# Weaving the q and k blocks of two attention layers between the attention steps

## The chip, the cores and the metric

The kernel runs on one core of one Trainium2 chip. The metric is device microseconds from the start to the end of one launch, and lower is better. TensorE (PE) multiplies matrices, VectorE (DVE) and ScalarE (ACT) work elementwise, GpSimd (POOL) issues the transfers of the small and streamed tables, and SyncE (SP) issues the transfers of the large weights. All data are float32.

## The reference

A transformer of two layers over 256 tokens of width 1024 is followed by a second network that the change does not touch. Each layer conditions its input, mixes tokens and runs a mixture of 32 experts:

```
mod = silu(c) @ ada_w[i] + ada_b[i]            # six rows of 1024: shift, scale, gate, twice
h   = rms_norm(x) * (1 + scale1) + shift1
q, k, v = split(h @ w_in, 3)                    # w_in is 1024 x 3072
y   = attention(q, k, v) @ w_out
x   = x + gate1 * y
h   = rms_norm(x) * (1 + scale2) + shift2
x   = x + gate2 * moe(h)                        # top 2 of 32 experts
```

Layer 0 uses differential attention: 8 heads, two softmax maps for each head, a chunk-causal mask, and 16 (head, query tile) pairs. Layer 1 uses stick-breaking attention with 16 heads: sigmoids and a reversed running sum of logarithms in place of a softmax.

## The kernel before

**Storage.** `ring` has six slots of 2 MB, and SP fills them in a written order; a slot is filled again when PE has counted its last use (`free(n)`). The eight 512-column slices of a layer's `w_in` and `w_out` are ring items 0 to 7 of the layer, behind them come the gate, up and down weights of the experts. `ada_in` holds three buffers of 1 MB for the rows of `ada_w` and `w_mod_2`. POOL loads them (`ada_load`, L1484), and they are called ada items here: items 0 to 31 belong to layer 0, items 32 to 63 to layer 1, eight items to a group. Item i can be loaded when the buffer of item i - 3 has been used.

**Groups of items.** In groups 1, 2, 5 and 6 (`SUMMED`) DVE multiplies each item by its column of `cond` and adds it to a running sum (`ada_sum`, L1851), and PE adds up the partitions once, at the group's last item. In the other groups PE multiplies each item itself (`ada_item`, L2181). When a group is through, `ada_take` adds the bias and POOL stores the row.

**Head (0 to 40 us).** SP loads the first 2048 columns of `ada_w` as eight pieces of 1 MB, with the constants and x behind the third, and then the weights. PE multiplies all eight pieces, turns `h`, and after `first_line` turns the row of shift and scale into columns (`first_norm`, L1864). ACT then writes `hT` (`take_hT`, L1659).

**q, k, v (`qkv`, L2215).** Twelve blocks of 16 matmuls: four of q, four of k, four of v. A block of q or k has two half blocks of 128 columns. ACT copies each block out of one of four banks (`take_qkv`, L1677). In the meantime DVE runs both sums of the layer. Only then do the attention steps begin.

**Attention steps.** `diff_attention` (L2275) runs 20 steps. Step k computes scores k, turns the probabilities of k - 3 and multiplies k - 4 by v, and twelve of the steps carry an ada item. `stick_attention` (L2317) runs 18 steps: scores k, running sums k - 1, product k - 2, with an item in 14 of them. Scores, exponentials and the division pass from PE to DVE (`diff_scores`, `diff_combine`, L1912) and ACT and back.

**Behind them.** `projection` (L2251) multiplies by `w_out` in four blocks of eight products; three items in layer 0 and two in layer 1 follow it, then come the turned x, the router (item 31 in layer 0) and the experts. SP holds back the experts' weights of layer 0 until 24 items are used, and the early down weights until 32 (layer 1: 64) are used. In layer 1 the context row of the second network is loaded by POOL when x is complete, and ACT squares it before the exponentials of the router.

## Time and profile before

| what | us |
|---|---|
| median of three runs (lowest, highest) | 1855.09 (1849.57, 1863.38) |
| the profiled execution, its span | 1853.06, 1851.3 |
| head, until the first block of q | 0 to 39.85 |
| q, k, v and both sums, layer 0 | 39.85 to 127.15 |
| attention steps, layer 0 | 127.15 to 185.04 |
| projection, layer 0 | 185.04 to 213.3 |
| its items, turned x, router | 213.3 to 243.12 |
| experts, layer 0 | 243.12 to about 727 |
| q, k, v, layer 1 | 733.81 to 827.67 |
| attention steps, layer 1 | 827.67 to 893.52 |
| projection, layer 1 | 893.52 to 921.78 |
| its items, turned x, router | 921.78 to 953.36 |
| experts of layer 1 with the second network, rest | 953.36 to 1851.3 |

The borders are starts of PE instructions in the trace. A row of the timeline gives the start, the time, the engine, the line of the kernel, the output and inputs, the number of instructions, and in brackets the idle time ahead of it with what ended it. L2179 is the helper that issues every matmul, so its rows are told apart by shape: 128x256 for half blocks, 128x512 with `ring` for v and the projection, `small` or `cst` with 128*1 or 128*2 for an ada item.

### The profile page before, as it was taken

The numbers are of one execution on the slowest core, as the hardware profiler recorded it, in microseconds if no ns is written. First come the engines' busy times: TensorE is split into PE (matmuls) and PEld (weight loads), VectorE is DVE, ScalarE is ACT, GpSimd is POOL, SyncE is SP. The second block draws the span as 40 slices with busy tenths as digits, with TensorE's granted clock in tenths as the row PEclk, the third lists the DMA queues.
The fourth block names the chain that finished last, engine by engine and source line by source line (L and its number), as shares of the span: only waits on it lengthen the run. The fifth ranks groups of instructions, "written<-read, shape, count | busy, mean of one in ns | idle before, by whom it ended". The sixth has DMA issues, their size and how long they took to land.

```text
span 1851.3 us, 18408 instructions
## 1 busy us (share of the span) xinstructions
PE 1687.5 (91%) x7485; PEld 858.7 (46%) x7485; DVE 489.6 (26%) x931; ACT 444.1 (24%) x939; POOL 158.1 (9%) x235
## 2 busy tenths in 40 slices
PE   5997999889888878989999999999998899989988
PEld 2843543333333334835464444444443356565564
DVE  1357220000000103244241002221120123553362
ACT  2015221111111102015231112334331034343351
POOL 2012010000000010113000010000000000100000
PEclk9998999999989999999989999999998999999999
DMA  9999779999999999987369989999999962413310
GB/s 348 360 350 401 277 278 419 421 421 420 421 421 419 420 413 397 338 349 239 109 259 389 369 298 404 393 414 420 420 420 409 377 230 100 148 53 117 137 46 24
DMA packets 119488, 585.12 MB, mean 316 GB/s; under 512 B 11744, under 2 KB 16680, under 8 KB 94720
## 3 DMA queue, kind: packets, MB, share of 16 engines
q1 hardware_dynamic: 97776, 489.59, 66.0%
q0 software_dynamic: 21504, 88.72, 13.1%
q10 hardware_dynamic: 112, 5.51, 0.8%
q8 instruction: 63, 1.03, 0.2%
q14 instruction: 33, 0.27, 0.0%
HBM read 578.87 MB, written 21.32 MB: 324 GB/s over the span
## 4 chain that ended last, share of the span: by engine, by line
PE 58%; DMA 29%; DVE 6%; ACT 3%; issue 3%; SPq 1%; ACTq 0%; DVEq 0%
PE psum L2179 55%; DMA ring<-in_expert_w_up 20%; DMA work<-in_ada_w 4%; DMA ring<-in_diff_w_in 2%; DVE work L1859 1%; PE psum L697 1%; DMA ring<-in_expert_w_gate 1%; DMA work<-in_ctx 1%; DMA work<-in_w_mod 1%; DVE small L1055 1%; PE psum L2418 1%; PE psum L1196 1%; DMA ring<-in_w_out 0%; DVE work L2147 0%; DVE work L2074 0%
## 5 line engine op out<-in xcount | busy, mean ns | idle before, releaser
L2179 PE MATMUL psum<-ring,work 128*64 128x512 f32 (+5 forms) x4272 | 1092.6, 574 | 69.6 <-DMA ring<-in_expert_w_up 56.3
L2179 PEld LDWEIGHTS psum<-ring,work 128*64 128x64 f32 (+2 forms) x4272 | 422.7, 152 | 666.1 <-issue 638.0
L2179 PE MATMUL psum<-work 128*128 128x192 f32 (+9 forms) x1048 | 220.4, 375 | 8.5 <-DVE work L2007 3.0
L2179 PEld LDWEIGHTS psum<-work 128*128 128x128 f32 (+3 forms) x1048 | 146.5, 191 | 108.0 <-issue 86.9
L2074 DVE TENSOR_TENSOR work<-work,psum 128x256 f32<-128x256 f32 x64 | 26.9, 421 | 593.2 <-ACT work L1779 593.2
L1779 ACT ACTIVATE work<-psum 128x256 f32<-128x256 f32 x64 | 24.5, 383 | 607.4 <-PE psum L2179 607.4
L2179 PE MATMUL psum<-work,ring 128*128 128x256 f32 x704 | 156.1, 381 | 3.5 <-DMA ring<-in_diff_w_in 2.0
L2179 PEld LDWEIGHTS psum<-work,ring 128*128 128x128 f32 x704 | 132.0, 190 | 27.8 <-issue 7.0
L1646 ACT ACTIVATE work<-psum 128x256 f32<-128x256 f32 (+5 forms) x184 | 79.7, 443 | 225.0 <-PE psum L2418 76.0
L1545 POOL DMA_INDIRECT expert_rows<-work,targets x56 | 55.1, 984 | 807.1 <-DVE work L2100 807.1
L2100 DVE TENSOR_TENSOR work<-psum,rows 128x512 f32<-128x512 f32 x64 | 44.3, 692 | 255.8 <-PE psum L2179 255.7
L1859 DVE SCALAR_TENSOR_TENSOR work<-work,small 128x2048 f32<-128x2048 f32 x28 | 65.8, 2352 | 80.2 <-DMA work<-in_ada_w 79.7
L1730 ACT ACTIVATE work<-psum,small 128x192 f32<-128x192 f32 x128 | 58.4, 506 | 25.5 <-PE psum L2179 25.5
L1646 ACT ACTIVATE ring<-psum 128x512 f32<-128x512 f32 (+2 forms) x54 | 34.5, 640 | 54.0 <-PE psum L2179 41.0
L2179 PE MATMUL psum<-work,cst 128*128 128x128 f32 (+4 forms) x176 | 30.2, 384 | 13.4 <-DVE work L2149 6.2
L697 PE MATMUL psum<-cst 128*128 128x256 f32 x166 | 42.2, 407 | 0.0
L1491 POOL DMA_DIRECT2D work<-in_ada_w x40 | 22.8, 574 | 215.5 <-DVE work L1859 162.1
L2179 PE MATMUL psum<-work,small 128*2 128x512 f32 (+1 forms) x256 | 38.2, 682 | 2.1 <-DMA work<-in_ada_w 1.2
L2418 PE MATMUL psum<-cst,work 128*128 128x128 f32 x128 | 27.3, 295 | 13.0 <-DVE work L2074 12.9
L697 PEld LDWEIGHTS psum<-cst 128*128 128x128 f32 x166 | 32.8, 205 | 12.0 <-issue 7.5
L1684 ACT ACTIVATE work<-psum 128x512 f32<-128x512 f32 x16 | 9.6, 597 | 104.9 <-PEq L2235 53.5
L1055 DVE TENSOR_REDUCE small<-psum 128x1 f32<-128x512 f32 (+1 forms) x48 | 28.7, 599 | 21.2 <-PE psum L2179 20.4
(293 smaller groups left out, 956.3 us busy)
## 6 DMA issues: line engine op xcount, KB each, us to landing
ring<-in_expert_w_gate SPq DMA_DIRECT2D x60, 2048.0 KB, 16.5
ring<-in_expert_w_up SPq DMA_DIRECT2D x60, 2048.0 KB, 17.2
ring<-in_expert_w_down SPq DMA_DIRECT2D x57, 2048.0 KB, 13.5
work<-in_ada_w POOLq DMA_DIRECT2D x40, 1024.0 KB, 8.0
ring<-in_w_in SPq DMA_DIRECT2D x12, 2048.0 KB, 8.8
work<-in_w_mod POOLq DMA_DIRECT2D x16, 1024.0 KB, 7.9
ring<-in_diff_w_in SPq DMA_DIRECT2D x6, 2048.0 KB, 38.2
ring<-in_sb_w_in SPq DMA_DIRECT2D x6, 2048.0 KB, 22.8
```

Of the source, the lines that this page charges most:

```text
L697: nc.tensor.matmul(bank[b][:, 0:S], ident, cst[:, 5 * P:7 * P], start=True, stop=True, skip_group_check=True)
L1055: V.tensor_reduce(nm2[:, k % 3:k % 3 + 1], score_bank(p, k)[:, 0:n * P], AX.X, ALU.max, negate=True).then_inc(sem("a_max"), 1)
L1491: pool.dma_start(ada_in[:, i % 3, 512 * k:512 * (k + n)], src[:, c * 512:(c + n) * 512].rearrange("(p t) n -> p t n", t=KT)[:, t, :]).then ...
L1545: pool.indirect_dma_start(expert_rows.rearrange("r (k n) -> (r k) n", k=2), bass.IndirectOffsetOnAxis(ap=targets[:, e:e + 1], axis=0), out ...
L1646: copy = lambda o_, i_: nc.scalar.activation(o_, i_, ACT.Copy)
L1730: ins = nc.scalar.activation(hS[:, c // QUAD % 2, t, 0:QUAD * LIST], bank[b][:, k * S:k * S + QUAD * LIST], ACT.Identity, scale=gain[:, t: ...
L1779: nc.scalar.activation(s_act, gu_bank(l, e)[:, 0:S], ACT.Silu).then_inc(sem("silu"), 1)
L1859: ins = V.scalar_tensor_tensor(now, now, cond[:, 0, t:t + 1], before, ALU.mult, ALU.add)
L2074: V.tensor_tensor(hid, s_act, gu_bank(l, e)[:, S:2 * S], ALU.mult).then_inc(sem("hid"), 1)
L2100: V.tensor_tensor(outb[:, e % 2, :], bank[down_bank(l, e)], gate2, ALU.mult).then_inc(sem("out_ev"), 1)
L2179: return T.matmul(out_, lhsT, rhs, start=start, stop=stop, skip_group_check=True)
L2418: ins = T.transpose(bank[2][:, j * P:(j + 1) * P], src[:, j * P:(j + 1) * P], ident)
```

## The change

- **Head.** x comes first. The first columns of `ada_w` come in two halves of their width, each in four pieces of two transfers (2 KB runs in place of 8 KB); between the halves SP loads the first four of eight row groups of the first two slices of v. PE makes the columns of half the row, starts all four v blocks with the first four products, and ends them with the second half of the row and of the weights.
- **Order.** The slices are loaded in the order v, v, q, k, q, k. Both layers compute v first, then the first pair of q and k blocks; the other 12 half blocks stand one at a time ahead of steps 0 to 11 of the attention. A step's scores wait for the pair that it needs.
- **Steps.** In layer 0 the steps 0 to 11 use one pair of score banks, turn probabilities 2 steps and multiply 3 steps after the scores; from step 12 it is two pairs, 3 and 4 steps as before. DVE combines k - 1 ahead of scores k up to step 12.
- **Items.** The first group of a layer (1, 5) is summed before the steps and used at step 0; the second (2, 6) is summed one item at a time in steps 1, 2, 4, 5, 7, 8, 10, 11 and used at step 12. Later items: 16 to 19 in steps 13 to 19, 20 and 21 behind them, 22 to 27 behind the first three projection blocks, 28 to 30 as before. Layer 1: 48 to 52 in steps 13 to 17, 53 behind them, 54 to 59 behind three projection blocks, 60 behind the fourth, then 61, 62, 63.
- **Waits.** The second pair of q and k slices waits until six items are used. POOL's first three item loads wait for the last piece of the head's row instead of for the first turned columns; in exchange the loads of lambda and of the router come later.
- **Places.** The turned result of layer 1 goes in the place of `h`, which keeps `hT` readable during the steps; layer 0's squares go back to their bank.

```diff
-    oT = hT
+    oT = hT, h.rearrange("p t d -> p (t d)").rearrange("p (k s) -> p k s", k=KT)
+    SLICES = (4, 5, 0, 2, 1, 3)
+    V_BLOCKS = (0, 2, 1, 3)
+    WOVEN = 12
+    WEAVE_BANK = (2, 5)
+    SUM_AT = (1, 2, 4, 5, 7, 8, 10, 11)
+    def diff_bank(u):
+        return 2 * (u % 2) if u >= WOVEN else 0
...
+            if l == 0 and n == 4:
+                sp.wait_ge(sem("ada_used"), 6)
...
+        sp.dma_start(x[:], a["x"][0].rearrange("(t p) d -> p t d", p=P)).then_inc(sem("x_in"), 16)
+        for a_ in range(2):
+            for q in range(4):
+                for t in range(2):
+                    sp.dma_start(first_in(a_, q)[:, t * 1024:(t + 1) * 1024].rearrange("p (s n) -> p s n", s=2),
+                                 first[:, 2 * q + t, :, a_, :]).then_inc(sem(f"first_in{4 * a_ + q}"), 16)
+                if a_ == 0 and q == 1:
+                    sp.dma_start(cst[:], a["consts"]).then_inc(sem("consts"), 16)
+            if a_ == 0:
+                for n in range(2):
+                    w = a["diff_w_in"][0][:, SLICES[n] * 512:(SLICES[n] + 1) * 512].rearrange("(t p) n -> p t n", t=KT)
+                    sp.dma_start(wslot(L_BASE[0] + n, KT, 512)[:, 0:4, :], w[:, 0:4, :]).then_inc(sem("w_first"), 16)
...
+        pool.wait_ge(sem("first_in7"), 32)
+        for i in range(3):
+            ada_load(i)
+        pool.wait_ge(sem("first_mm"), 2)
...
-            for g in SUMMED[2 * l:2 * l + 2]:
-                ada_sum(g)
-                ada_take(g)
+            ada_sum(SUMMED[2 * l])
...
                 for k in range(16 + 2):
-                    if k == 11:
-                        ada_take(3)
+                    if 1 <= k <= WOVEN:
+                        diff_combine(k - 1)
                     if k < 16:
                         diff_scores(k)
-                    if k >= 2:
+                    if k >= WOVEN + 2:
                         diff_combine(k - 2)
+                    if k == 1:
+                        ada_take(1)
+                    if k in SUM_AT:
+                        ada_sum(2, [SUM_AT.index(k)])
+                    if k == WOVEN:
+                        ada_take(2)
...
             router_prep(l)
+            ada_take((3, 7)[l])
             update_x(2 * l, "proj_mm", v)
...
+        def woven_half(l, p, c):
+            j = (p - 4) // 2
+            out_ = bank[WEAVE_BANK[l] + p % 2][:, c * S:(c + 1) * S]
+            n = L_BASE[l] + 2 + p % 2 + 2 * (j // 2)
+            if c == 0:
+                loaded(pe, n)
+                pe.wait_ge(sem("qkv"), EACH["qkv"] * l + ((2, 4)[p % 2] if p < 6 else p - 1))
+            w = wslot(n, KT, 512)
+            col = j % 2 * 256 + c * P
+            for t in range(KT):
+                ins = mm(out_, w[:, t, col:col + P], hT[:, t, :], t == 0, t == KT - 1)
+            if c:
+                if j % 2:
+                    taken(ins, n)
+                else:
+                    ins.then_inc(sem("qkv_mm"), 1)
...
+        def head():
+            first_product(0, range(0, 4))
+            first_turn(range(0, 6))
+            first_product(0, range(4, 6))
+            keep_warm(0, 2)
+            first_product(0, range(6, KT))
+            first_cols(0)
+            keep_warm(0, 5)
+            for i, b in enumerate(V_BLOCKS):
+                v_part(0, b, range(0, 4))
+                if i == 0:
+                    first_turn(range(6, KT))
+                elif i == 1:
+                    first_product(1, range(0, KT))
+                elif i == 2:
+                    first_cols(1)
+        def front(l, ts):
+            for i, b in enumerate(V_BLOCKS):
...
+            for p in (4, 5):
+                for c in range(2):
+                    woven_half(l, p, c)
...
-        DIFF_ITEMS = share_out(16, [0, 0] + 8 * [1] + [0, 0] + 4 * [1, 0])
+        DIFF_ITEMS = [[KT - 1] if k == 0 else [2 * KT - 1] if k == WOVEN else [(k + 19) // 2] if k in (13, 15, 17, 19) else []
+                      for k in range(16 + 4)]
+        STICK_ITEMS = [[5 * KT - 1] if k == 0 else [6 * KT - 1] if k == WOVEN else [35 + k] if k > WOVEN else []
+                       for k in range(HEADS_S + 2)]
+        PROJ_ITEMS = [[22, 23], [24, 25], [26, 27], []], [[54, 55], [56, 57], [58, 59], [60]]
...
             for k in range(16 + 4):
+                if k < WOVEN:
+                    woven_half(0, 6 + k // 2, k % 2)
...
-            for i in (28, 29, 30) if l == 0 else (62, 63):
+            for i in (28, 29, 30) if l == 0 else (61, 62, 63):
                 ada_item(i)
```

## Rows read from the trace of the kernel before

**Rows 1.** The page, part 4: shares of the chain that ended last, by engine.

```profile
PE 58%; DMA 29%; DVE 6%; ACT 3%; issue 3%; SPq 1%; ACTq 0%; DVEq 0%
```

**Rows 2.** Stretches: us, busy (count) of PE, PEld, DVE, ACT, POOL; PEclk, DMA, GB/s.

```profile
0.00:39.85 39.85, 19.17 (x111) 7.94 (x111) 4.13 (x12) 8.53 (x16) 7.53 (x17) 1.00 0.94 338
...
39.85:80.00 40.15, 39.28 (x180) 33.98 (x181) 15.40 (x7) 3.77 (x7) 4.91 (x9) 1.00 1.04 392
...
127.15:160.20 33.05, 24.75 (x161) 10.46 (x161) 26.71 (x71) 18.52 (x83) 9.81 (x18) 0.85 0.98 378
...
185.04:213.30 28.26, 27.96 (x67) 12.33 (x68) 3.95 (x7) 2.73 (x4) 0.00 (x0) 1.00 0.70 261
...
280.00:699.00 419.00, 362.21 (x1590) 142.54 (x1586) 36.58 (x69) 44.69 (x106) 30.80 (x33) 0.96 1.01 419
...
893.52:921.78 28.26, 27.96 (x66) 12.33 (x67) 3.68 (x6) 2.73 (x4) 0.00 (x0) 1.00 0.00 1
```

**Rows 3.** Timelines of PE and POOL: start, us, engine, line, operation [idle before].

```profile
33.72 1.04 PE L2179 MATMUL psum<-ring,small 128*1 128x512 f32 x8
...
37.10 1.61 POOL L1491 DMA_DIRECT2D work<-in_ada_w  x3
```

**Rows 4.** Timeline of DVE, first layer: sums of one group, scores two steps apart.

```profile
44.97 1.29 DVE L1861 TENSOR_SCALAR work<-work,small 128x2048 f32<-128x2048 f32 x1 [8.12 <-DMA work<-in_ada_w]
...
81.42 2.35 DVE L1859 SCALAR_TENSOR_TENSOR work<-work,small 128x2048 f32<-128x2048 f32 x1 [4.82 <-DMA work<-in_ada_w]
...
132.66 0.42 DVE L1918 SCALAR_TENSOR_TENSOR work<-cst,psum 128x256 f32<-128x256 f32 x1
...
160.22 0.42 DVE L1918 SCALAR_TENSOR_TENSOR work<-cst,psum 128x256 f32<-128x256 f32 x1
```

**Rows 5.** Timeline of PE inside the steps of the first attention.

```profile
144.04 0.42 PE L2294 MATMUL psum<-cst,work 128*128 128x128 f32 x2 [0.86 <-DVE work L1934]
...
144.61 1.04 PE L2179 MATMUL psum<-work,small 128*1 128x512 f32 x8
...
145.58 0.70 PE L2179 MATMUL psum<-work 64*128 64x256 f32 x4
...
146.38 0.62 PE L2179 MATMUL psum<-work 128*128 128x128 f32 x4
...
148.64 0.49 PE L2179 MATMUL psum<-work 64*128 64x128 f32 x4
```

**Rows 6.** The chain of waits: start, us, what.

```profile
91.68 5.02 DMA work<-in_ada_w
...
214.66 12.35 DMA work<-in_w_mod
...
923.84 14.94 DMA work<-in_ctx
```

**Rows 7.** DMA issues of 140 to 190 us: count, KB, median us to landing.

```profile
work<-in_w_mod POOLq DMA_DIRECT2D x7, 1024.0 KB, 13.6
```

**Rows 8.** Timeline of SP's DMA issues.

```profile
153.75 0.34 SPq L1442 DMA_DIRECT2D ring<-in_expert_w_gate  x1
```

**Rows 9.** Timeline of PE, second layer: first block, then inside the steps.

```profile
733.81 14.15 PE L2179 MATMUL psum<-work,ring 128*128 128x256 f32 x64
...
846.95 0.92 PE L2179 MATMUL psum<-work 64*128 64x256 f32 x4
...
847.80 1.14 PE L2179 MATMUL psum<-work,cst 128*128 128x256 f32 x6
...
848.87 0.86 PE L2179 MATMUL psum<-work 128*64 128x256 f32 x4
...
866.36 1.14 PE L2179 MATMUL psum<-work,cst 128*128 128x256 f32 x6 [0.91 <-DVE work L2149]
...
870.32 1.14 PE L2179 MATMUL psum<-work,cst 128*128 128x256 f32 x6 [1.18 <-DVE work L2149]
...
873.16 0.92 PE L2179 MATMUL psum<-work 64*128 64x256 f32 x4
```

More of the change, by code:

```diff
@@ L1619, in _, with stick_act @@
         pool_second(pool)
-    def stick_act(act, link, copy):
+    def stick_act(act, link, copy, take_woven):
         act.preload_act_table_set("natural_log_exp_and_others")
+        for p in range(6):
+            take_woven(1, p)
         for k in range(HEADS_S + 2):
+            if k < WOVEN and k % 2:
+                take_woven(1, 6 + k // 2)
             if k < HEADS_S:
@@ L1795, in _ @@
             take_hT(2 * l)
-            take_qkv(l)
             if l == 0:
                 act.preload_act_table_set("natural_log_exp_and_others")
+                for p in range(6):
+                    take_woven(0, p)
                 act.wait_ge(sem("lam_dot"), 1)
@@ L1812, in _ @@
             else:
-                stick_act(act, link, copy)
+                stick_act(act, link, copy, take_woven)
             square_norm(2 * l + 1)
@@ L1849, in gain_cols, with ada_sum @@
             link(V.scalar_tensor_tensor(gain, gain, 1.0, g_, ALU.add, ALU.mult))
-        def ada_sum(g):
-            for t in range(KT):
+        def ada_sum(g, ts=range(KT)):
+            for t in ts:
                 i = KT * (g - 1) + t
@@ new lines, in first_product @@
+        def first_product(a_, ts):
+            for t in ts:
+                if t % 2 == 0:
+                    pe.wait_ge(sem(f"first_in{4 * a_ + t // 2}"), 32)
+                for k in range(4):
+                    ins = mm(bank[7][32 * k:32 * k + 1, a_ * S:(a_ + 1) * S], cond[:, 0, t:t + 1],
+                             first_in(a_, t // 2)[:, t % 2 * 1024 + k * S:t % 2 * 1024 + (k + 1) * S], t == 0, t == KT - 1)
+                if t % 4 == 3:
+                    ins.then_inc(free(2 * a_ + t // 4), 1)
@@ new lines, in first_turn, with first_cols @@
+        def first_turn(ts):
+            for t in ts:
+                for tile in range(TT):
+                    ins = T.transpose(bank[FIRST_TURN[t // 2]][:, (t % 2 * TT + tile) * P:(t % 2 * TT + tile + 1) * P],
+                                      h[:, tile, t * P:(t + 1) * P], ident)
+                if t % 2:
+                    ins.then_inc(sem("hT_mm"), 1)
+        def first_cols(a_):
+            pe.wait_ge(sem("first_line"), 2 * a_ + 1)
+            for i in range(2):
+                ins = T.transpose(bank[(3, 5)[a_]][:, i * P:(i + 1) * P], line[:, a_ * S + i * P:a_ * S + (i + 1) * P], ident)
+            ins.then_inc(sem("first_mm"), 1)
@@ new lines, in v_part, with taken @@
+        def v_part(l, b, ts):
+            w = wslot(L_BASE[l] + b % 2, KT, 512)
+            for t in ts:
+                if b == 0:
+                    pe.wait_ge(sem("hT_done"), HT_AT[2 * l] + t + 1)
+                ins = mm(bank[b][:], hT[:, t, b // 2 * P:(b // 2 + 1) * P], w[:, t, :], t == 0, t == KT - 1)
+            return ins
+        def taken(ins, n):
+            ins.then_inc(free(n), 1)
+            pe.wait_ge(free(n), turn_of(n) + 1)
+            pe.sem_inc(sem("qkv_mm"), 1)
+        def woven_half(l, p, c):
+            j = (p - 4) // 2
+            out_ = bank[WEAVE_BANK[l] + p % 2][:, c * S:(c + 1) * S]
[10 more added lines that the diff above has]
+                    taken(ins, n)
+                else:
+                    ins.then_inc(sem("qkv_mm"), 1)
@@ L2263, in projection @@
                     mm(bank[5][:, 0:NG + NX], C["ones"], kT[:, 2, 0:NG + NX], True, True).then_inc(sem("r_bias"), 1)
+                for n in PROJ_ITEMS[l][i]:
+                    ada_item(n)
             for hf in range(2):
@@ L2308, in diff_attention @@
                     ada_item(i)
+            for i in (20, 21):
+                ada_item(i)
             for j in range(4):
@@ L2562, in _ @@
                 transpose_h(2)
-            qkv(l)
+            front(l, range(0 if l else 4, KT))
             (diff_attention, stick_attention)[l]()
             projection(l)
-            for i in (28, 29, 30) if l == 0 else (62, 63):
+            for i in (28, 29, 30) if l == 0 else (61, 62, 63):
                 ada_item(i)
```

262 lines of the change are left out of this document (123 added, 139 removed).

## The prediction, made before the change was run

> **What bounds the kernel now.** I read the page's chain first: PE is 58% of what ended last and transfers 29% [rows 1]. So the same microsecond can belong to either, and it has to be asked stage by stage. The windows [rows 2] give the stages. The experts of layer 0 run at DMA share 1.01 and 419 GB/s while PE has 57 us idle in 419: that stage is paced by transfers, but its stream is tied to slots that PE frees, so it moves with the moment at which the experts begin. Ahead of it the stretch from 39.85 to 80 is full on both sides (PE 39.28 of 40.15 busy, DMA 1.04). The attention steps of layer 0 are full on neither: in 127.15 to 160.20 PE is busy 24.75 of 33.05 us with a mean clock of 0.85, so stretches of it run at the lower of the two levels, 1.2 GHz, behind idle time. That is the room the change aims at. The projection is PE alone: 27.96 of 28.26 us in both layers, with DMA 0.70 in the first and 0.00 in the second.
>
> **Units.** A block of q or k: 64 matmul records of four half blocks take 14.15 us, with the gap to the next some 14.2, so a half block is 3.55 us [rows 9]. One ada item holds PE for 0.97 us (144.61 to 145.58) [rows 5]. Two steps of the first attention hold PE, without the item, for 0.57 + 0.80 + 0.62 + 0.49 = 2.5 us, 1.24 a step [rows 5], while before they came 2.76 us apart (132.66 to 160.22 is ten steps) [rows 4]. In layer 1 a step holds PE for 0.85 + 1.07 + 0.79 = 2.71 us without its item, and two steps without an item came 3.96 apart (866.36 to 870.32), PE waiting 1.18 for DVE [rows 9].
>
> **Head, layer 0.** The first v products can start about ten us earlier, since half of the 4+4 MB of `ada_w` now suffices. That isn't what counts: the steps can't begin before group 1 is summed. POOL issued its first three loads at 37.10, 3.4 us behind PE's last head product [rows 3]. Now they wait for the last piece itself, which has 2.1 MB of v ahead of it: at 392 GB/s 5.4 us later, about 39.1. So the sums start 2 us later than at 44.97; they ended at 81.42 + 2.35 = 83.8 [rows 4]. Against this, SP has only 6.3 MB queued beside them, since the second pair of slices waits for six items. All that must have landed is some 27 MB (x 1.0, constants 0.9, the row 8.4, v 4.2, first q and k 4.2, eight items 8.4), and the old kernel had moved 13.5 + 15.7 = 29.2 MB by 80 us [rows 2], 27 by 75. The end of the sums thus lies between 77 and 86; I take 80, and 81.3 with item 7. PE has finished v, the first q and k blocks and one half block by then (28.4 + 14.2 + 3.55 from about 29, held up by weights), and idles in front of item 7. This idle time and the smaller transfers are not free: 1.5 us for the clock is set down below, between 0 and 4.
>
> **Woven steps, layer 0.** Step 1 starts at 81.3. Eleven steps hold PE for 3.55 + 1.24 = 4.8 us each. DVE needs about 2.4 us for scores and combination, 2.76 by the old pace as a bound, and 2.35 for a sum in eight of twelve steps: 5.1 in such a step, 4.3 in the mean, below PE's 4.8. I take PE's: 52.8, plus the 1.5. Step 12 starts at 135.6. From the scores of u = 12, at 160.2 before, to the projection at 185.04 it was 24.8, with 0.5 for PE's part 25.3. The end of the attention is then 160.9, **24 us earlier**.
>
> **What goes the other way.** Six of the items that stood in steps, 22 to 27, now stand in the projection: 5.8 us. This leaves 18.3. These items also wait for transfers. An item's load can't be issued before the third last is used, and what it takes depends on company: 5.02 us alone at 91.68, 12.35 beside the two expert loads behind the projection [rows 6], a median of 13.6 beside four expert loads and the 5.4 MB of expert rows [rows 7]. Those four loads went out at 153.75, 31 us ahead of the projection [rows 8], because 24 items were used; now item 23 is behind the first projection block, so they start in it, together with the expert rows and eight items: 5.4 + 8.4 + 7.3 MB, then 4.2 + 4.2 more, 29.5 MB or 70 us at 419 GB/s from 161 on. Followed block by block with 8 to 15 us for a load, PE waits 1 us at item 25, 5 at 27, 4 at 30, less for shorter loads: 3 to 11 us, I take 8. The experts' weights are in by 231 to 235, just when they are wanted. **Layer 0: 24 - 6 - 8 = 10 us.**
>
> **Layer 1.** v takes 28.4 and the first pair 14.2 from 733.81: 776.4. Item 39 is ready by then: DVE begins its group when the last rows of layer 0 are added, before 734, and eight sums took 38.8 us in layer 0. Step 0 is 3.55 + 0.85 + 0.97, step 1 is 3.55 + 0.85 + 1.07, ten steps of 6.26: 850. There ACT's and DVE's chain of 3.96 fits under 6.26, and even with a sum in DVE's queue. From step 12 to the projection it was 873.16 to 893.52, 20.4 us; with two more items and the wait for the last sum 23.5. The projection starts at 873.5, **20 us earlier**. Six items in it cost 6: its end comes 14 us earlier. Here DMA is idle, so their loads come in time at 5 us.
>
> The exception is the last. Item 60 now stands behind the fourth block, and the load of item 63 waits for it. It goes out about 1.6 us after the projection's end, beside the two expert loads that this end releases. That is the very company of the load that took 12.35. So PE is held until 14 us behind the projection, done at 14.9; before, its two items were done after 2.1. The turned x and the router stand behind. Of these 12.8 us some 1.7 are free, since the router's end was waiting for the context row (923.84, 14.94 us [rows 6]) and ACT's work on it (from the projection to the first expert layer 1 took 31.6 us, layer 0 with two more items 29.8). The cost is 11 (between 4 with a load of 5.02 and 14 with one of 14.94, that of the context row). **Layer 1: 14 - 11 = 3 us.**
>
> **Other edits,** each at nothing. Turning layer 1's results into h's place: the same ACT copy. Squares in PSUM: same count. The loads of lambda, router and norm rows come later but are wanted at 80 and 160; if norm rows came behind 168 the projection's bias product would wait. SP's twelve extra issues lie ahead of transfers that are queued anyway. 2 KB runs: up to 1 us in the head.
>
> **Sum.** 10 + 3 = 13 us off the profiled execution's 1853.06 gives 1840; this lies 2 us under the median of the runs, so I say **1842**. Under 1%, 18.5 us, a measurement of this kernel can't well tell from no change.
>
> **Rivals.**
> - **The items' loads don't hold PE.** If they land in about 5 us even in company, layer 0 keeps 18.3 - 3 = 15 and layer 1 14 - 4 = 10: 25 us, 1830. For it speaks the 5.02 us of a load without company [rows 6] and that three loads can be under way; against it the 12.35 and the median of 13.6 [rows 6, 7].
>  The Trainium skill ("DMA: Bandwidth & Descriptors", section "Queues, rings and completion order") says that each DMA engine takes turns between the queues that have work, a packet at a time; by that, 1 MB on POOL's queue beside SP's would be in after about 2 MB, near 5 us. The 12.35 us of the trace [rows 6] do not agree.
> - **The half blocks lengthen the steps (slower).** PE's queue is in order, and so is DVE's: a late half block holds the next scores, a late sum the next combination. If nothing overlaps, a step lasts 3.55 + 2.76 = 6.3 in layer 0 and 3.55 + 3.96 = 7.5 in layer 1: 11 x 1.5 + 10 x 1.25 = 29 us; with half of the 16 sums of 2.35 in series 19 more: 1890. It makes the kernel slower by over 1% once a step grows by more than (13 + 18.5) / 21 = 1.5 us. Against it: scores k + 1 need only DVE's scores k, a half block earlier.
> - **Transfers set the end.** If the experts' stream, and not PE, decides when layer 0 goes on, its later start (behind item 23) gives all 10 us back, and late loads the other 3: 1855. Against it: the old stream was idle for 0.30 of the projection [rows 2], which the new order fills.
>
> **Chances.** Forecast 0.56, short loads 0.23, longer steps 0.09, transfers 0.12. The range 1825 to 1859 takes in the third rival, most of the first, and the bounds of head (-3 to +6) and stalls (-12 to +6); outside lie the slow rival and the lower end of the first. Faster by over 1%: 0.21 of the first rival and 0.06 of the forecast's low end, 0.27. Slower: 0.07 of the slow rival. Within: 0.66.
>
> **What would show it.** DVE's last sum of group 1 at 78 to 83; half blocks 4.8 us apart in layer 0 and 6.3 in layer 1, PE at 1.00 there; the first projection at 161; items 25, 27 and 30 each behind a DMA wait, and one wait of over 10 us for `w_mod` behind the second projection. It would be wrong if the sums end after 86, if step distances exceed 5.5 and 7, or if item 63 waits under 5 us.

## The result: slower by 0.8%, and the profile after

| | us |
|---|---|
| kernel before, median of 7 runs (lowest, highest) | 1855.09 (1849.57, 1863.38) |
| changed kernel, median of 7 runs | 1868.04 (1866.37, 1873.02) |
| ratio, 95% interval | 1.0078 (1.0062 to 1.0093) |
| profiled execution of the changed kernel, its span | 1866.77, 1865.0 |

The forecast was 1842 us, with a range of 1825 to 1859. The span grew by 13.7 us instead of shrinking by 13. Against the table of before, from the trace of after:

| stage | start before | start after | forecast |
|---|---|---|---|
| projection, layer 0 | 185.04 | 169.45 | 160.9 |
| first expert, layer 0 | 243.12 | 253.69 | 233 |
| v, layer 1 | 733.81 | 743.71 | |
| projection, layer 1 (from v) | 893.52 (159.7) | 889.08 (145.4) | (139.7) |
| first expert, layer 1 | 953.36 | 966.42 | |

So layer 0 was 15.6 us ahead at its projection and 10.6 behind at its experts: 26 us went between the two, a stretch that took 58.1 us before and takes 84.2 now. From v to the first expert layer 1 took 222.7 us, before 219.6: another 3. Behind that nothing changed (898.6 us to the end, before 897.9). These are two single executions. Two kernels below differ from the changed one in layer 1 alone, and their traces have the projection of layer 0 at 173.64 and 171.81 and the first expert at 258.92 and 257.50, so a start in layer 0 is only good to some 5 us; the stretch from projection to first expert is steadier (84.2, 85.3 and 85.7).

The page's chain, shares by engine; it answers to [rows 1] and hardly tells the two kernels apart:

```profile
PE 62%; DMA 28%; DVE 4%; SPq 2%; issue 2%; ACT 2%; POOL 0%; ACTq 0%; DVEq 0%
```

The windows of the changed kernel (columns as in [rows 2]): the head's second part, two slices of it, woven steps, projection with its items in layer 0, PE's longest hole in it, the experts, projection with its items in layer 1.

```profile
39.85:80.00 40.15, 30.26 (x88) 16.83 (x87) 13.95 (x10) 6.20 (x10) 8.78 (x15) 0.89 0.94 311
...
60.00:70.00 10.00, 7.40 (x33) 6.00 (x32) 2.10 (x1) 1.20 (x2) 0.53 (x1) 1.00 0.94 234
70.00:80.00 10.00, 2.87 (x7) 2.31 (x8) 5.12 (x3) 0.00 (x0) 1.06 (x2) 0.57 0.67 217
...
91.30:127.00 35.70, 35.09 (x182) 28.09 (x179) 26.53 (x49) 13.78 (x57) 4.25 (x7) 1.00 0.59 215
...
169.45:226.70 57.25, 41.23 (x139) 14.58 (x139) 6.01 (x8) 3.68 (x5) 5.49 (x10) 0.85 0.98 382
...
186.60:197.68 11.08, 0.00 (x1) 0.00 (x2) 1.08 (x1) 2.73 (x4) 0.55 (x1) 0.70 0.97 367
...
280.00:699.00 419.00, 367.62 (x1622) 145.61 (x1618) 37.04 (x71) 46.44 (x110) 31.81 (x34) 0.96 1.01 417
...
889.08:936.60 47.52, 39.30 (x151) 14.22 (x147) 6.00 (x8) 4.17 (x7) 9.93 (x18) 0.93 0.71 274
```

Three things stand here. The stretch to 80 us was full on both sides before (39.28 of 40.15, 392 GB/s [rows 2]) and now has 30.26 and 311. The woven steps are what the change was meant to give: PE 35.09 of 35.70 at clock 1.00, with DMA only 0.59 busy, so bandwidth is left over there. And the projection of layer 0 is the reverse: PE 41.23 of 57.25 at 0.85 with DMA 0.98. The work that transfers do was not spread with the work that PE does.

PE's timeline, layer 0: the k block (48 products in one row), half blocks in steps, then the projection with the waits at its items 25 and 27.

```profile
77.13 12.87 PE L2241 MATMUL psum<-work,ring 128*128 128x256 f32 x48 [9.43 <-DMA ring<-in_diff_w_in]
...
109.85 3.62 PE L2241 MATMUL psum<-work,ring 128*128 128x256 f32 x16
...
114.53 3.62 PE L2241 MATMUL psum<-work,ring 128*128 128x256 f32 x16
...
169.45 7.13 PE L2241 MATMUL psum<-ring,work 128*128 128x512 f32 x16 [1.21 <-ACT work L1763]
...
197.68 1.89 PE L2241 MATMUL psum<-work,small 128*2 128x512 f32 x8 [11.08 <-DMA work<-in_w_mod]
199.50 7.95 PE L2241 MATMUL psum<-ring,work 128*128 128x512 f32 x16
...
213.05 1.89 PE L2241 MATMUL psum<-work,small 128*2 128x512 f32 x8 [4.63 <-DMA work<-in_w_mod]
214.86 8.79 PE L2241 MATMUL psum<-ring,work 128*128 128x512 f32 x16
```

Behind each wait PE runs "cold", at the lower of its two clock levels for a while: the granted clock is 0.50 in the item right behind each wait (197.68 to 199.50 and 213.05 to 214.86), which takes 1.8 us for 1.0, and 0.89 and 0.81 over the blocks that follow, which take 7.95 and 8.79 us for 7.13. Item 30 (in the row 223.96) has no wait. DVE's timeline, the fifth and the last of the eight sums of group 1, which answer to the 81.42 of [rows 4]; the chain of waits in both projections, which answers to [rows 6]; and the DMA issues of 170 to 200 us (columns as in [rows 7]):

```profile
70.35 2.35 DVE L1909 SCALAR_TENSOR_TENSOR work<-work,small 128x2048 f32<-128x2048 f32 x1 [8.25 <-DMA work<-in_ada_w]
...
86.86 2.35 DVE L1909 SCALAR_TENSOR_TENSOR work<-work,small 128x2048 f32<-128x2048 f32 x1 [4.92 <-DMA work<-in_ada_w]
```

```profile
186.93 26.08 DMA work<-in_w_mod
...
225.32 12.72 DMA work<-in_w_mod
...
882.30 4.92 DMA work<-in_w_mod
...
925.11 9.57 DMA work<-in_w_mod
```

```profile
work<-in_w_mod POOLq DMA_DIRECT2D x4, 1024.0 KB, 23.1
ring<-in_expert_w_gate SPq DMA_DIRECT2D x2, 2048.0 KB, 25.9
ring<-in_expert_w_up SPq DMA_DIRECT2D x2, 2048.0 KB, 33.0
```

A load of 1 MB took 5.02 us alone and 13.6 in the old crowd [rows 6, 7]; in the new one the median of four is 23.1. That of item 25, issued at 178.03, was in when PE went on at 197.68, after 19.65 us; that of item 27, issued at 186.93, was in 26.08 us later, but it had item 26's ahead of it on POOL's own queue. Who had the DMA engines meanwhile stands in the queues of 178 to 198 us (packets, MB, share): ACT's with the expert rows, SP's, and POOL's with the items.

```profile
q10 hardware_dynamic: 67, 2.92, 40.3%
q1 hardware_dynamic: 175, 2.61, 34.6%
q0 software_dynamic: 179, 1.33, 18.3%
```

POOL's queue has as many packets through as SP's (179 and 175), but 7.4 KB in each against 15, and 44 for ACT's. So it moves 1.33 MB of 6.86, 67 GB/s. ACT's count is lower because its copy runs out in this window. While all three had work, in 183 to 188 us, the three counts are near equal:

```profile
q10 hardware_dynamic: 21, 1.20, 65.5%
q1 hardware_dynamic: 25, 0.41, 27.0%
q0 software_dynamic: 22, 0.18, 11.7%
```

POOL has 36 GB/s there. With ACT's copy out of the way, in 193 to 203 us, it is 193 packets of SP's and 188 of POOL's, and POOL has 138 GB/s, or 7.6 us for an item. PE takes two items per block there, one in 4.5 us. Last, PE in layer 1: the wait at item 53, the projection, and item 63.

```profile
887.26 1.89 PE L2241 MATMUL psum<-work,small 128*2 128x512 f32 x8 [3.88 <-DMA work<-in_w_mod]
889.08 7.90 PE L2241 MATMUL psum<-ring,work 128*128 128x512 f32 x16
...
934.72 1.89 PE L2241 MATMUL psum<-work,small 128*2 128x512 f32 x8 [8.22 <-DMA work<-in_w_mod]
```

### The profile page after: what moved, and what is told of

Same layout as the page of the kernel before. It is cut to its first block, busy times and chain, and to the rows that moved or that the text cites. A ratio compares the mean times of both kernels' runs of the same rounds, so it can differ in the third digit from the quotient of the medians.

```text
span 1865.0 us, 18564 instructions
## 1 busy us (share of the span) xinstructions
PE 1684.4 (90%) x7537; PEld 858.5 (46%) x7537; DVE 488.6 (26%) x935; ACT 446.2 (24%) x939; POOL 158.1 (8%) x236
## 3 DMA queue, kind: packets, MB, share of 16 engines
q0 software_dynamic: 21536, 88.72, 12.9%
q8 instruction: 64, 1.05, 0.2%
## 4 chain that ended last, share of the span: by engine, by line
PE 62%; DMA 28%; DVE 4%; SPq 2%; issue 2%; ACT 2%; POOL 0%; ACTq 0%; DVEq 0%
PE psum L2241 58%; DMA ring<-in_expert_w_up 20%; DMA work<-in_w_mod 3%; DMA ring<-in_diff_w_in 2%; PE psum L713 1%; SPq L1416 1%; DMA ring<-in_expert_w_gate 1%; DMA ring<-in_expert_w_down 1%; DVE small L1071 1%; PE psum L2555 1%; PE psum L1212 1%; DMA mod_scratch<-rows 0%; SPq L1406 0%; DMA ring<-in_w_out 0%; SPq L1447 0%
## 5 line engine op out<-in xcount | busy, mean ns | idle before, releaser
L2241 PE MATMUL psum<-work,ring 128*128 128x256 f32 x704 | 161.4, 385 | 10.0 <-DMA ring<-in_diff_w_in 9.4
L2555 PE MATMUL psum<-cst,work 128*128 128x128 f32 x128 | 27.3, 295 | 13.0 <-DVE work L2127 12.9
L713 PE MATMUL psum<-cst 128*128 128x256 f32 x154 | 38.1, 402 | 0.0
L1696 ACT ACTIVATE work<-x 128x1024 f32<-128x1024 f32 x10 | 10.5, 1055 | 109.5 <-DVE x L1954 93.9
```

The source lines that it names most:

```text
L713: nc.tensor.matmul(bank[b][:, 0:S], ident, cst[:, 5 * P:7 * P], start=True, stop=True, skip_group_check=True)
L2241: return T.matmul(out_, lhsT, rhs, start=start, stop=stop, skip_group_check=True)
L2555: ins = T.transpose(bank[2][:, j * P:(j + 1) * P], src[:, j * P:(j + 1) * P], ident)
```

## The experiments

The kernel before was timed anew beside each group of kernels: 1854.79, 1855.07, 1853.84 and 1856.14 us. The ratios below, with their 95% intervals, are to those, and 1.0078 (1.0062 to 1.0093) is the changed kernel's.

**1. Only the six items moved, in the kernel before.** Items 22 to 27 leave the steps and stand behind the first three projection blocks of layer 0; nothing is woven.

```diff
-        DIFF_ITEMS = share_out(16, [0, 0] + 8 * [1] + [0, 0] + 4 * [1, 0])
+        DIFF_ITEMS = share_out(16, [0, 0] + 6 * [1] + 12 * [0])
+        PROJ_ITEMS = [[22, 23], [24, 25], [26, 27], []], [[], [], [], []]
```

> The kernel before the change with one part of it: items 22 to 27 of layer 0 stand behind the first three projection blocks in place of in the attention steps, and group 3 is taken behind the steps; so SP's wait for 24 items ends in the projection too. Theory (moving these items costs more than it gives, because their loads meet the experts' weights and rows): six items of 1 us and waits of 12 to 20 us in the projection, against some 5 us less in the steps: 10 to 20 us slower than before, 1865 to 1875. Rival (the cost comes only from attention ending earlier while the transfers are not further on): under 6 us, 1855 to 1861.

Measured: 1874.18, 1.0103 (1.0085 to 1.0121). PE's timeline in the projection:

```profile
207.51 1.89 PE L2179 MATMUL psum<-work,small 128*2 128x512 f32 x8 [9.32 <-DMA work<-in_w_mod]
...
222.91 1.89 PE L2179 MATMUL psum<-work,small 128*2 128x512 f32 x8 [4.31 <-DMA work<-in_w_mod]
```

The waits of the changed kernel are there without any weaving. The move alone costs 19 us, as expected: from the projection to the first expert it is 82.8 us for 58.1, and the steps that it empties give back only 4 (projection at 181.04 for 185.04). In the changed kernel the woven half blocks earn part of it back.

**2. The same products, hardly any bytes.** In the changed kernel the loads of items 22 to 30 carry 64 columns of each piece of up to 2048; the rest of these rows is left out.

```diff
+                wide = 64 if 22 <= i <= 30 else n * 512
-                pool.dma_start(ada_in[:, i % 3, 512 * k:512 * (k + n)],
+                pool.dma_start(ada_in[:, i % 3, 512 * k:512 * k + wide],
```

> The changed kernel, with the loads of items 22 to 30 cut to 64 of 512 columns in each section, one eighth of their bytes; it leaves out most of those rows of w_mod, while the products, waits and signals stay as they are. It separates the price of the transfers from that of the items' products on PE. Theory (PE waits 11.08 and 4.63 us at items 25 and 27 for bytes, and its blocks behind them run cold for another 2 to 3 us): both waits fall under 2 us and the time is 1848 to 1855 us. Rival (what holds PE is that only three buffers stand between an item and its load, so latency and POOL's turn decide, not bytes): the wait at item 25 stays above 6 us and the time at 1862 to 1868.

Measured: 1849.73, 0.9975 (0.9959 to 0.999), 18 us under the changed kernel. One number in the expectation is off: the trace shows that 32 KB were left of 1024, not one eighth.

```profile
work<-in_w_mod POOLq DMA_DIRECT2D x6, 32.0 KB, 6.4
```

PE's wait at item 25 fell from 11.08 to 1.76 us and the one at 27 vanished. The first expert starts at 237.15, 16.5 us earlier than in the changed kernel and 6 before the old one. From the projection to the first expert it is 58.1 us in the kernel before, 84.2 in the changed one and 66.9 here. So 17.3 of the 26.2 us lost were paid for bytes, with products, buffers and POOL's order all in place; 5.8 are the six items' products, and 3 are left, about what PE waits at items 25 and 31 (1.76 and 1.68). Small loads are not free in this crowd either: those of 32 KB took 6.4 us. This kernel also changes the size of POOL's packets and leaves their number, and the counts stay equal beside SP's queue (186 to 190 us):

```profile
q1 hardware_dynamic: 51, 0.84, 56.7%
q0 software_dynamic: 52, 0.03, 2.7%
```

**3. The crowd thinned from either end.** SP's wait for 24 items ahead of the experts' weights is taken out (first kernel); or the 5.4 MB of expert rows go out at step 2 of the attention instead of ahead of the projection (second); or the first, and `w_out` waits for 8 items instead of 13 (third).

```diff
-            if l == 0:
-                sp.wait_ge(sem("ada_used"), KT * 3)
...
+                    if k == 2:
+                        act.dma_start(expert_rows, finite).then_inc(sem("rows_set"), 16)
...
-                sp.wait_ge(sem("ada_used"), KT * 2 - 3)
+                sp.wait_ge(sem("ada_used"), KT)
```

> The changed kernel without SP's wait for 24 used items ahead of the experts' weights of layer 0. Theory (the loads of the moved items hold PE in the first projection, because four expert loads and the expert rows start in it; item 25 waited 11.1 us and item 27 4.6 us): the four expert loads go out from about 127 us on, into the stretch where DMA was only 0.59 busy, the two waits shrink to under 8 us in sum and the kernel gets 6 to 12 us faster than the changed one (1868): 1856 to 1862. Rival (the three item buffers alone set the pace of the items, whatever else is queued): the waits stay over 12 us and the time stays at 1866 to 1870.

> The changed kernel with ACT's copy of 5.4 MB into expert_rows issued at step 2 of the first attention (about 97 us) in place of right before the first projection. Theory: it leaves the crowded stretch, 13 us of DMA time less there; the waits at items 25 and 27 fall by 5 to 12 us: 1856 to 1863. Rival (SP's four expert loads alone are enough to fill the stretch, and the copy only takes what is left over): under 3 us, 1865 to 1870. If the sums of group 2 wait for transfers because of it, the woven steps grow beyond 4.7 us.

> The changed kernel without the wait for 24 items ahead of the experts' weights, and with w_out already behind 8 used items instead of 13. The first of these alone moved the crowd to steps 12 to 19 (waits of 1.5 to 3.5 us at six items, projection 18.5 us later) and won nothing. Theory (layer 0 ends where the transfers end: 20 MB must pass between 127 us and the experts, while DMA is only 0.59 busy from 91 to 127): w_out and the first two expert loads now pass in that gap, 8.4 MB or 20 us of transfers leave the crowd, and the experts start 8 to 18 us earlier: 1850 to 1860. Rival (the waits of the items come from three buffers and not from company): no gain, 1866 to 1872.

Measured: 1871.54 (1.0097, 1.0077 to 1.0116), 1868.17 (1.0081, 1.006 to 1.0101) and 1861.63 (1.0041, 1.0026 to 1.0057). The first two gained nothing against the changed kernel, and the third gained 6.4 us, less than the 8 to 18 expected. In the first, the four loads went out at 126 to 140 and met items 16 to 21 instead; two of PE's six waits in and behind the steps, and the one left in the projection:

```profile
160.15 1.89 PE L2239 MATMUL psum<-work,small 128*1 128x512 f32 x8 [3.55 <-DMA work<-in_ada_w]
...
167.52 1.89 PE L2239 MATMUL psum<-work,small 128*1 128x512 f32 x8 [3.49 <-DMA work<-in_ada_w]
...
210.51 1.89 PE L2239 MATMUL psum<-work,small 128*2 128x512 f32 x8 [5.39 <-DMA work<-in_w_mod]
```

Its projection starts at 187.98, 18.5 us later than in the changed kernel. In the second the wait at item 25 is gone, but in the steps from 110 to 127 PE is busy for only 13.40 of 17 us (17.00 in the changed kernel), and 4.27 us at item 27 stay. Its projection starts 4.75 later than the changed kernel's, which is no more than single executions differ by. In the third the loads go out from 91 us on, into the woven steps, where the changed kernel had DMA at 0.59. There PE reads nothing from POOL's queue except sums for DVE, which have slack.

**4. Two places outside the projection.** POOL issues the router's loads at item 9 instead of item 4 (first); item 60 stands behind the third block of layer 1's projection, so that item 63's load goes out a block earlier (second); and both (third).

```diff
-                if i == 4:
+                if i == 9:
                     router_load(0)
...
-        PROJ_ITEMS = ..., [[54, 55], [56, 57], [58, 59], [60]]
+        PROJ_ITEMS = ..., [[54, 55], [56, 57], [58, 59, 60], []]
```

> The changed kernel with the loads of the first router (runs of 16 to 128 bytes) behind item 9 in place of item 4. Theory (these short runs hold the DMA engines between 60 and 70 us, where DMA moves 234 GB/s at share 0.94, so that item 4's load takes 15 us and k's first slice lands only at 77.1): the sums of group 1 end at 80 to 85 in place of 89.2, the woven steps start 4 to 9 us earlier, the kernel is 2 to 8 us faster: 1860 to 1866. Rival (the total of bytes and three buffers set the end of the sums): they end at 88 to 90, no difference.

> The changed kernel with item 60 behind the third projection block of layer 1 in place of behind the fourth, so that the load of item 63 can start 7 us earlier, before the two expert loads. Theory: the wait of 8.2 us at item 63 goes, and with it the cold clock behind it: 7 to 11 us faster, 1857 to 1861. Rival (the router then waits for the context row and ACT as before the change): 3 us or less, 1865 to 1868.

> The changed kernel with only the two repairs that won alone: item 60 behind the third block (9.8 us) and the router's loads behind item 9 (7.4 us). They sit in different layers; the sum is expected: 1848 to 1854, equal to before or a little faster. If layer 0's gain were only a shift that the transfers take back, 1856 to 1860.

Measured: 1860.67 (1.0031, 1.0016 to 1.0046), 1858.26 (1.0021, 1.0008 to 1.0034), 1854.51 (0.9996, 0.9982 to 1.001). Windows of the first, for the two slices shown above of after, and PE behind layer 1's projection in the second:

```profile
60.00:70.00 10.00, 7.51 (x33) 6.01 (x32) 2.47 (x2) 1.19 (x2) 0.53 (x1) 1.00 0.89 289
70.00:80.00 10.00, 6.70 (x22) 5.60 (x23) 6.73 (x3) 0.00 (x0) 1.05 (x2) 0.66 0.72 246
```

```profile
929.87 2.76 PE L2241 MATMUL psum<-work,small 128*2 128x512 f32 x24 [0.30 <-PE psum L2241]
```

The router's four loads of 2 to 128 KB stood on POOL's queue right behind item 4's. Later, the same ten microseconds move 289 GB/s for 234, k's slice is in at 73.30 for 77.13, and the last sum ends at 86.4 for 89.2, not at 80 to 85 as expected. The rate is no accident of one trace: all seven traces of kernels with these loads at item 4 have 230 to 259 GB/s in 60 to 70 us, and all nine with them at item 9 have 289 to 309. How 2.8 us at the sums become 7 in the end was not followed. With item 60 earlier the 8.22 us wait is gone, and from the projection of layer 1 to its first expert it is 66.6 us for 77.3. The two gains (7 and 10 us) add up to 13.5, not 17.

**5. All of these together** (`w_out` and the experts' weights early, router late, item 60 earlier), and then variants of it. In the second kernel the expert rows go out on ACT's queue behind the first norm. In the third POOL also issues the loads of items 21 and 53 ahead of its wait for the scratch rows; in the fourth, items 22, 23 | 24 | 25, 26, 27 stand behind the projection blocks.

```diff
+                if n == 1 and t == 0:
+                    act.dma_start(expert_rows, finite).then_inc(sem("rows_set"), 16)
...
-                if g > LAST0 * l and i % 8 == 4:
+                if g > LAST0 * l and i % 8 == (5 if g in (2, 6) else 4):
                     stored(g)
...
-        PROJ_ITEMS = [[22, 23], [24, 25], [26, 27], []], ...
+        PROJ_ITEMS = [[22, 23], [24], [25, 26, 27], []], ...
```

> g_wout together with item 60 behind the third block (alone 9.8 us) and the router's loads behind item 9 (alone 7.4 us). Theory: the three repairs sit in different stretches (layer 1's projection, group 1's sums, the crowd of layer 0) and add up: 1832 to 1843, faster than before. Rival (layer 0 ends where its transfers end, so two repairs of layer 0 overlap): router and w_out together give no more than the larger: 1840 to 1850.

> The kernel of the last combination (router loads late, w_out and the experts' weights early, item 60 earlier) gave 1850.6 us and still waits 5.09 us for the load of item 25 in the first projection, with a cold block behind it. The 5.4 MB of expert rows go out just ahead of that projection. Here they go out on ACT's queue about 12 us later, behind the first norm, where that kernel's DMA was about half busy. Theory (company on the queues sets how long a w_mod load takes): the wait at item 25 falls to under 1 us, its block runs warm, 1843 to 1848 us. Rival (the crowd just moves, as it did when the experts' weights went early): a wait of 3 us or more appears at items 27 to 31 or at the router instead, 1849 to 1853.

> As the kernel with late expert rows, and POOL issues the store and the bias and norm loads of groups 2 and 6 one item later, so that the loads of items 21 and 53 go out first (before, POOL waits 8.66 us for the scratch rows ahead of item 53's load, and PE waits 4.38 at item 21 and 4.04 at item 53). Theory: POOL's order of issue is what delays them; both waits fall under 1 us and the time goes 4 to 8 us below that kernel: 1837 to 1843. Rival (item 21's load is late because of company alone, and behind item 53 something else is late by as much): 0 to 3 us less.

> As the kernel before it in this call, with items 22, 23 | 24 | 25, 26, 27 behind the first three projection blocks of layer 0 instead of 22, 23 | 24, 25 | 26, 27: item 25 has one block (7 us) longer for its load. Theory: what is left of the wait at item 25 goes and nothing comes at 27, since the loads ahead of it are issued when items 22 to 24 are done: 0 to 5 us less than that kernel. Rival: the wait only moves to item 26 or 27, because loads 26 and 27 are issued when 23 and 24 are used and 24 is no earlier: no difference within 0.1%.

Measured: 1850.59 (0.9977, 0.9967 to 0.9986), 1865.46 (1.0051, 1.0033 to 1.0069), 1860.87 (1.0028, 1.0013 to 1.0044) and 1860.4 (1.0034, 1.0021 to 1.0047). The first missed its 1832 to 1843: its repairs meet each other in the steps from 127 to 140, where PE is busy for 8.24 of 13 us at 402 GB/s (11.73 with only the weights early). Late rows were wrong: the wait at item 25 went and this came, at items 28, 29 and 31 of the second kernel:

```profile
209.55 1.04 PE L2240 MATMUL psum<-work,small 128*2 128x512 f32 x8 [1.45 <-DMA work<-in_w_mod]
...
224.78 1.89 PE L2240 MATMUL psum<-work,small 128*2 128x512 f32 x8 [14.20 <-DMA work<-in_w_mod]
...
232.12 1.89 PE L2240 MATMUL psum<-work,small 128*2 128x512 f32 x8 [5.46 <-DMA work<-in_w_mod]
```

Items 28 to 30 are the last before the router, and have no block between them to hide a load; item 29's load, issued at 200.50, had the expert rows beside it and then two expert loads of 2 MB (208.22). The queues of 194 to 214 us:

```profile
q10 hardware_dynamic: 96, 5.51, 77.0%
q0 software_dynamic: 283, 1.86, 23.2%
```

POOL's order in the third takes 4.6 us off the second, near what was expected of it, though its total was missed with the base: from v to layer 1's projection it is 141.8 us for 145.8. The places of the items in the fourth change nothing while that hole stands.

**6. POOL's order and item 25, each alone.** The move of item 53's load in the changed kernel (first) and in the combination (second); item 21's as well (third); the second with the items in the places 22, 23 | 24 | 25, 26, 27 (fourth). The edits are those above, with `g == 6` in place of `g in (2, 6)` where it is item 53 alone.

> The changed kernel, with one edit in layer 1: POOL issues the load of item 53 ahead of its wait for the scratch rows of group 6 and the bias, norm and gate loads behind them, not after. Theory: POOL's order alone holds item 53 for 3.88 us and runs the block behind it cold (7.90 for 7.13), so layer 1's projection starts 4 to 5 us earlier and the time is 1862 to 1865 us. Rival: the norm and gate rows that now come later are what the step behind waits for, or the load of item 54 is late instead: 1866 to 1869.

> The best kernel so far (router loads late, w_out and the experts' weights early, item 60 earlier: 1850.6 us) with that same edit in layer 1. It waits 4 us at item 53. Theory: 4 to 6 us less, 1845 to 1847, below the kernel before by 0.4 to 0.6%. Rival as above: 1849 to 1852.

> As the kernel before it in this call, and the same move for group 2 in layer 0, so that item 21's load goes out ahead of POOL's wait for the scratch rows (PE waits 4.38 us at item 21 there). Theory: the wait falls under 1.5 us and what is gained stays, 1841 to 1844. Rival (what layer 0 gains ahead of its projection it gives back at item 25, whose load then starts earlier into the same crowd): within 1.5 us of the kernel before it.

> As the kernel with the edit in layer 1 alone, with items 22, 23 | 24 | 25, 26, 27 behind the first three projection blocks of layer 0 instead of 22, 23 | 24, 25 | 26, 27. Item 25 then has one block, 7.1 us, longer for its load, and waits 5.09 us without that. Theory (item 25 only lacks time): its wait goes, items 28 to 30 are ready as before, 3 to 5 us less than that kernel, 1840 to 1843. Rival (all loads behind 25 are issued later too, since load 28 follows item 25): the wait comes back at items 28 to 30, within 1.5 us of that kernel or slower.

Measured: 1865.53 (1.0045, 1.003 to 1.0061), 1847.3 (0.9949, 0.9935 to 0.9963), 1847.54 (0.9954, 0.9941 to 0.9967) and **1840.46 (0.9911, 0.9895 to 0.9926)**. In the changed kernel the place of item 53's load in POOL's order gave 2.5 us by the medians and 6 by the two ratios, so its size there stays open; in the trace the wait of 3.88 us became 3.23, and the stretch from v to the projection 143.7 us for 145.4. In the combination the wait of 4.12 became 2.04, no cold block follows, and the stretch is 142.0 us for 145.5. All ten traces with the old order have 144.1 to 145.8 there, and the five combinations with the new one 141.8 to 142.6. So the order is worth some 3 us, but it did not hold the load alone: in the second kernel it goes out at 873.00, right when item 50 is used (871.63), and PE still waits for it until 879.43. Item 21's place gave nothing, as the rival had it: PE then waits 4.86 us at item 24 and 1.13 at item 25. Item 25 lacked time: with one block more, it is 65.5 us from the projection to the first expert for 73.5. PE in the projection of the second kernel, then of the fourth:

```profile
198.24 1.89 PE L2239 MATMUL psum<-work,small 128*2 128x512 f32 x8 [6.42 <-DMA work<-in_w_mod]
200.06 8.68 PE L2239 MATMUL psum<-ring,work 128*128 128x512 f32 x16
```

```profile
201.14 1.90 PE L2239 MATMUL psum<-work,small 128*2 128x512 f32 x16
...
204.50 1.04 PE L2239 MATMUL psum<-work,small 128*2 128x512 f32 x8 [1.46 <-DMA work<-in_w_mod]
```

6.42 us and a cold block of 8.68 became 1.46 us in front of item 27, and no item behind waits. The last kernel beats the one before by 0.9% and, by the two ratios, the changed one by 1.7%. The same move gave nothing with the expert rows late: then items 28 to 31 set the end, and item 25 does not.

## Why the prediction was wrong, step by step

**Right.** The woven steps of layer 0 hold PE for what the rows gave: half blocks of 3.62 us, distances of 4.6 (109.85 to 114.53 to 119.12), forecast 4.8, at clock 1.00. In layer 1 the distance is 6.36, forecast 6.26. The waits at item 27 (4.63 us, forecast 5) and at item 63 stand where they were put. That at item 25 was 11.08 for a forecast of 1, and the 4 us at item 30 did not come. The experts' stream is 417 GB/s at 1.01 and moved with its start. The rival of longer steps did not come. That of short loads is what experiment 2 made true by hand for layer 0: even then the kernel is only 4 us under the one before, since the head, and layer 1 with its wait at item 63, stay as they are.

**Head, failed: 80 against 89.2.** The step reckoned that "all that must have landed is some 27 MB" and took the old rate for it. The changed kernel had moved 26.5 MB by 80 us (352 and 311 GB/s), the old one 29.2. The rate fell to 234 GB/s in 60 to 70 at a share of 0.94, and the share to 0.67 behind it. The router's loads, which I set at nothing because they are "wanted at 80 and 160", are 2.8 us of the 9.2 at the sums and 3.8 at k's slice (experiment 4). The other 6 were not tried one by one. The share of 0.67 says that loads were not issued in time: SP's second pair of slices waits for items, and POOL's loads for DVE's sums, each of which waits for its load. This is an argument from the rows, and no run tested it.

**The load's duration, failed: this is the largest.** "Followed block by block with 8 to 15 us for a load" came from the 13.6 us of the old crowd [rows 7], though the same paragraph had put four expert loads more, the expert rows and the items into the same 70 us. Item 25's load took 19.65 us and item 27's 26.08. The waits are 11.08 + 4.63, the two cold blocks another 2.5 and the two cold items 1.7: 19.9 us where 8 stood and 11 was the bound. (The forecast's own three waits, 1 + 5 + 4, already add up to 10.)

What was missing is how three queues share. I had read the Trainium skill ("DMA: Bandwidth & Descriptors", section "Queues, rings and completion order") as if turns gave each queue the same bytes, and set it aside because the trace had 12.35 for 5. It says that a turn is a packet. The packets of the trace differ in size, and by their counts the rule holds in the stretches read here in which the queues had work throughout: 21, 25 and 22 for three queues and 193 to 188 for two in the changed kernel, 51 to 52 in experiment 2, where POOL's packets are a small part of their size. It holds in the kernel before too. The load of 12.35 us, issued at 214.66, had this company in 218 to 224 us:

```profile
q1 hardware_dynamic: 120, 1.70, 66.4%
q0 software_dynamic: 103, 0.84, 33.4%
```

Ahead of that, from 214 to 218 us, only SP's packets passed, 82 of them: some 3 us of the 12.35 lie between the issue and POOL's first packets. For item 25 the bytes can be counted: in 178 to 198 us passed its own 1.05 MB with 0.28 of its neighbours' on POOL's queue, 2.61 MB of SP's and 2.92 of ACT's, 6.86 MB at 343 GB/s. With the expert rows taken out of the way (experiment 3, second), the median load of 175 to 200 us is 12.5 us and the wait at item 25 is gone. The wait at item 27 stays, since 7.6 us for an item beside SP alone is still slower than PE uses them. Against all this stands what a load may last unseen: item 25's went out at 178.03 and was wanted at 186.60, 8.6 us later, with one block between.

**Layer 0, sum.** Forecast 10 us gained, measured 10.6 lost: 8.5 at the projection's start, 12.4 behind it (26.2 for 13.8). Of the 8.5, step 1 was 10 us late (91.3 for 81.3, the head), the steps to the twelfth took 50.6 us for 54.3, and the rest 27.5 for 25.3. The 5.8 us for the six items' products were right at full clock; experiment 2 bears out that most of the rest was bytes.

**Layer 1, sizes off.** Counted from v, its projection starts 14.3 us earlier, forecast 20. The woven steps were not the cause: step 12 starts 115.2 us behind v (858.92), forecast 116.2. From there to the projection it is 30.2 us where I had 23.5: 3.88 at item 53, 0.85 for that item at clock 0.50, and 1.8 in waits for the last sum and for items 48 and 49. The 23.5 had the wait for the sum but none for an item's load, and I had not followed POOL through its wait for the scratch rows (8.66 us from 867.96). The six items' loads in the projection do come in time, as written. Item 63 was sized right in part by luck. From the projection to the first expert it is 17.5 us more, forecast 17.1. But PE was done with item 63 12.9 us behind the projection where 14.9 stood, its load having taken 9.57 us for 12.35, and the 1.7 us of slack did not show. Experiment 4 confirms the place: 10 us for one item moved by one block.

**The slow side.** Its one rival lay in the steps. None put the slow end in the projection, though this stretch held the largest unknown, and the rival of transfers stopped at no change. Of the 27 us between the forecast and the trace, 8.5 lie ahead of layer 0's projection, 12 behind it and 6 in layer 1, all to the slow side.

## What to carry to other kernels

When work moves from one stage to another, its loads move too: before pricing the move, write down for each stage the bytes on all queues and what is left of the share of 1.0, not only what the moved work costs the engine. Streamed operands with few buffers belong where the bandwidth is idle, or get a stretch of other work as long as the load takes in that company. A load's time alone is not its time in company: count the packets of each queue that is busy with it, and the operand's own queue, whose loads follow one another. A crowd doesn't vanish by an earlier or later issue, it meets what runs there; it is worth moving only into a stretch whose own loads have slack.

## What the runs showed of the hardware

- While queues were busy together, the numbers of their packets came out near equal, so the queue with the smallest packets got the fewest bytes: 21, 25 and 22 packets moved 1.20 MB on ACT's queue, 0.41 on SP's and 0.18 on POOL's (183 to 188 us of the changed kernel). A load of 1 MB took 5.02 us alone, 12.35 beside SP's queue, 19.65 beside both (item 25's, with the last packets of item 24's ahead of it).
- POOL's queue moved 36 GB/s beside both others and 138 beside SP's alone.
- A load of 32 KB in that company still took 6.4 us.
- Four loads of 2 to 128 KB went with a rate of 234 GB/s in a window at a share of 0.94, and 289 at 0.89 without them: a high share doesn't say that bytes flow.
